# Gate and up weights of the thirty-first expert, asked for as 120 and 8 partitions

## What is computed

```python
h = rmsnorm(x, g_ffn).reshape(b * t, d)          # d = 1024
...                                               # top group, then top-2 experts in it
def add_expert(acc, params):
    wg, wu, wd, c = params                        # (1024, 512), (1024, 512), (512, 1024), float32
    act = jax.nn.silu(h @ wg) * (h @ wu)
    return acc + (act @ wd) * c[:, None], None
out, _ = lax.scan(add_expert, jnp.zeros_like(h), (w_gate, w_up, w_down, combine))
```

## Time and profile before

| | us |
|---|---|
| median of three runs | 1108.88 |
| lowest, highest | 1107.67, 1110.88 |
| the profiled execution | 1107.98 |
| its span, first to last instruction | 1106.2 |
| PE busy (share of the span) | 1052.4 (95%) |
| VectorE, ScalarE, GpSimd busy | 440.0, 235.6, 302.5 |
| HBM read, written | 290.09 MB, 29.72 MB |

### The profile page before, as it was taken

The page is one execution under the profiler, slowest core; times in us unless marked ns, Lnnn a source line. Parts: engine busy times, 40 slices in busy tenths (PEclk is TensorE's granted clock), DMA queues, the critical chain, the costliest instruction groups (busy, mean ns, idle before and its releaser), DMA issues. The chain is left out here.

```text
span 1106.2 us, 17768 instructions
## 1 busy us (share of the span) xinstructions
PE 1052.4 (95%) x6801; PEld 610.0 (55%) x6801; DVE 440.0 (40%) x1210; ACT 235.6 (21%) x545; POOL 302.5 (27%) x262
## 2 busy tenths in 40 slices
PE   6999999999999999899999999999999999988896
PEld 3644444445777777433565555555555555545453
DVE  3555888888566565523344311111111111111222
ACT  2113221122444446411021101111111111111011
POOL 1023422551554444103000112222222222222222
PEclk9999999999999999999999999999999999999999
DMA  6230232207576344897895799999999999999993
GB/s 211 92 117 21 77 106 96 94 13 273 152 237 221 118 137 141 328 387 251 336 414 201 280 357 417 413 419 414 415 413 416 417 412 415 415 417 417 418 406 123
DMA packets 85497, 304.39 MB, mean 275 GB/s; under 512 B 23453, under 2 KB 27677, under 8 KB 73507
## 3 DMA queue, kind: packets, MB, share of 16 engines
q1 hardware_dynamic: 67682, 273.47, 63.4%
q0 software_dynamic: 9824, 16.98, 5.3%
q10 hardware_dynamic: 7904, 12.78, 3.1%
HBM read 290.09 MB, written 29.72 MB: 289 GB/s over the span
## 5 line engine op out<-in xcount | busy, mean ns | idle before, releaser
L413 PE MATMUL p_z<-k_w,k_xT 128*128 128x512 f32 (+2 forms) x528 | 209.0, 550 | 0.0
L413 PEld LDWEIGHTS p_z<-k_w,k_xT 128*128 128x128 f32 (+1 forms) x528 | 92.3, 189 | 102.9 <-issue 101.7
L876 PE MATMUL a_G<-k_xT,k_w 128*128 128x260 f32 x512 | 125.9, 390 | 0.0
L2035 ACT ACTIVATE k_rows<-e_Y,x_share 64x512 f32<-64x512 f32 x64 | 43.7, 682 | 329.8 <-PE e_Y L1916 329.4
L876 PEld LDWEIGHTS a_G<-k_xT,k_w 128*128 128x128 f32 x512 | 92.2, 190 | 26.2 <-issue 13.6
L2122 DVE SCALAR_TENSOR_TENSOR k_rows<-e_G,x_share,k_rows 128x256 f32<-128x256 f32 x32 | 15.5, 484 | 228.9 <-ACT k_rows L2030 228.9
L971 POOL TENSOR_TENSOR k_x<-k_x 128x512 f32<-128x512 f32 x64 | 80.5, 1271 | 87.4 <-DVE k_side L1037 67.7
L2162 POOL DMA_INDIRECT out_y_p<-k_rows,x_table x32 | 46.2, 1444 | 176.9 <-ACT k_rows L2035 176.9
L166 POOL DMA_INDIRECT k_rows<-token_rows,x_halves x32 | 33.8, 1056 | 174.1 <-PE e_TX L1896 159.5
L1896 PEld LDWEIGHTS e_TX<-k_c,k_rows 64*64 64x64 f32 x1024 | 64.0, 212 | 13.1 <-issue 12.5
L1896 PE MATMUL e_TX<-k_c,k_rows 64*64 64x64 f32 x1024 | 68.4, 283 | 0.0
(11 more groups left out here) (375 smaller groups left out, 1549.2 us busy)
## 6 DMA issues: line engine op xcount, KB each, us to landing
k_w<-in_w_in SPq DMA_DIRECT2D x11, 2048.0 KB, 8.2
k_w<-in_w_gate SPq DMA_DIRECT2D x8, 2048.0 KB
k_w<-in_w_up SPq DMA_DIRECT2D x8, 2048.0 KB
k_xT<-in_w_down SPq DMA_DIRECT2D x8, 2048.0 KB, 27.7
k_oT<-in_w_gate SPq DMA_DIRECT2D x8, 2048.0 KB
k_side<-in_w_up SPq DMA_DIRECT2D x8, 2048.0 KB
x_page<-in_w_down SPq DMA_DIRECT2D x8, 2048.0 KB
x_w_out<-in_w_gate SPq DMA_DIRECT2D x8, 2048.0 KB
```

Source lines behind the costliest of these rows:

```text
L413: last = nc.tensor.matmul(z[u % 3][0:p, 0:WIDTH[k]], s.xT[:, j, 128 * i:128 * i + p], s.w[:, c % 2, j, 0:WIDTH[k]], start=j == 0, stop=j = ...
L876: last = nc.tensor.matmul(G[u % 2][:, 0:HT], s.w[:, q % 2, j, 128 * c:128 * c + 128], s.xT[:, j, HT * h:HT * h + HT], start=j == 0, stop=j ...
L2035: last = nc.scalar.activation(y[j][:, W * h:W * h + W], Y[j][CAP * h:CAP * h + CAP, :], ACT.Copy, scale=s.share[CAP * h:CAP * h + CAP, 0, ...
```

## The change

The thirty-first expert's gate and up weights are each asked for with two DMAs, one for partitions 0 to 119 and one for partitions 120 to 127. All other weights are asked for as before. The semaphore of the place gets 32 rather than 16 for that load, and `weights_in` adds the difference to the total that PE waits for. No byte more or less is moved, and the arithmetic is the same.

```diff
+PARTITIONS = ([slice(0, 128)], [slice(0, 120), slice(120, 128)])
+IN_FIFTEENTHS = ((NE - 2, 0), (NE - 2, 1))
+
+
 def load_expert(eng, io, s, e, n):
 
     r = e % DEPTH[n]
     for b, part in s.ew[n][r]:
-        eng.dma_start(part, s.expert(io[EXPERT_WEIGHTS[n]], e, n)[:, b:b + part.shape[1], :]).then_inc(s.ew_in[n][r], 16)
+        rows = s.expert(io[EXPERT_WEIGHTS[n]], e, n)[:, b:b + part.shape[1], :]
+        for p in PARTITIONS[(e, n) in IN_FIFTEENTHS]:
+            eng.dma_start(part[p], rows[p]).then_inc(s.ew_in[n][r], 16)
     if (n, r) == (2, FIRST):
         load_down_last(eng, io, s, e, s.ew_in[n][r])
...
 def weights_in(s, e, n):
 
     r, parts = e % DEPTH[n], len(s.ew[n][e % DEPTH[n]]) + 2 * ((n, e % DEPTH[n]) == (2, FIRST))
-    return s.ew_in[n][r], 16 * (FIRST_LOADS.get((n, r), parts) + parts * (e // DEPTH[n]))
+    parts_more = len(s.ew[n][r]) * ((e, n) in IN_FIFTEENTHS)
+    return s.ew_in[n][r], 16 * (parts_more + FIRST_LOADS.get((n, r), parts) + parts * (e // DEPTH[n]))
```

## The result

| | before | after |
|---|---|---|
| median, us (runs) | 1108.82 (4) | 1126.18 (4) |
| lowest, highest | 1107.67, 1110.88 | 1122.32, 1127.43 |
| the profiled execution | 1107.98 | 1122.32 |
| its span | 1106.2 | 1120.5 |

The change makes the kernel slower: the ratio after to before is 1.0148, 95% interval 1.0132 to 1.0165, or +17.4 us by the medians. Within the two profiled executions it is +14.3 us of span; that of after was the fastest of its four runs (the others took 1125.25 to 1127.43 us). The forecast was 1107.1 us with a range up to 1110.8.

The account below looks back on a forecast made before the run. The prediction took the slowest DMA engine's end in a full queue as the bound. A gain of 1.8 us, other terms 0, gave 1108.88 - 1.8 = 1107.1 us, range 1105.1 to 1110.8.

Parts of the forecast that it names:

- What bounds the kernel: DMA engines full from about 665 us; the slowest, about 2.4 us behind the second slowest, sets the end.
- What one partition costs: Cut gate and up loads: 0.63 us per partition; one engine spared 10.1 us, eight engines loaded 1.26 us more.
- If the spared engine is the slowest (case a): At the end of the queue, the spared engine was last: 1.1 to 2.4 us gained, 1.8 taken; chance 0.45.
- case (b): At the end of the queue, the slowest engine gets an extra partition: +1.3 us, 1110.1 us; chance 0.25.
- More instructions on SP: Two added DMA issues on SP: 0 us taken, 0 to 0.7 us if the cover is gone.
- The wait: PE waits for 16 more on two semaphores it already waits on, for the same bytes: 0 us.
- Two descriptors of completion more, and the start of small transfers: Cut loads in the full queue: between 0 and 0.63 us each, 0 taken.
- The rule against the cut: Advice of one 128-partition transfer; by it alone the cut loads would cost 1.26 us and win nothing.
- Few engines (case d): 120 partitions go to eight engines: 1119 us, share about 0.5, wait before `e_U<-x_merged` over 5 us; chance 0.07.
- The chances: For the whole kernel's measured time against before: faster 0.04, same 0.88, slower 0.08.

Follow-up runs that it names:

- e5_expert_14: The change's 120 and 8 cut on the gate and up weights of expert 14 instead of 30, against the kernel before: 1123.38 us, ratio 1.0139.
- e8_first_eight: Kernel before plus one 1 MB HBM-to-HBM copy in 8 rows behind the up load of expert 30: 1113.23 us, ratio 1.0046.
- e1_120_only: The change without its 8-partition DMAs, so partitions 120 to 127 are not loaded, against the kernel before: 1126.64 us, ratio 1.0164.
- e12_8_slices: Kernel before with the same two tensors each loaded by eight DMAs of all 128 partitions, one 2 KB row per partition each: 1108.97 us, ratio 1.0011.
- e11_2_slices: Kernel before with the same two tensors each loaded by two DMAs of all 128 partitions, rows 0-3 and 4-7: 1108.86 us, ratio 0.9997.
- e13_eight_4_apart: Kernel before with only partitions 0 to 63 of the two tensors loaded, by eight DMAs each of 8 partitions 4 apart: 1108.79 us, ratio 0.9999.

## Why the prediction was wrong, point by point

**What bounds the kernel.** Right. The rate of the full DMA queue sets the time from 665 us on, and `e5_expert_14` shows how strictly: a loss there 300 us before the end arrives at the end with 15.0 us. But the prediction went on from "a spread of engines at the end" to "that is what this change can act on". The change acted on the rate, which the prediction had fixed.

**What one partition costs.** This is the step that failed. It took 26.0 GB/s for an engine, whatever partitions it writes, and so 0.63 us for a partition. In the trace of after a busy engine has 219 / 16 = 13.7 GB/s and a partition takes 1.19 us, for 30 us. It was read from rows in which every transfer was of all 128 partitions, and no row of before showed another kind. A bound on both sides was called for: an upper end of twice the time for the two tensors alone would have been 1108.88 + 10.1 = 1119.0 us, and since the neighbours in the queue slow down too (30 us at 220 GB/s are 6.6 MB, and the two tensors are 4.2 MB), even that end is short of 1126.2.

**If the spared engine is the slowest (case a).** Wrong as the likeliest case. `e8_first_eight` places the last engine among the eight that get the extra partition, so case (b) had the right place. Its price was to be 1.3 us; of that nothing was seen, as after (1126.18 us), with the 8-partition DMAs, is no slower than `e1_120_only` (1126.64), though noise of this size could hide 1.3 us. The 17.4 us are another mechanism, and the prediction had no case for it.

**More instructions on SP.** Right: 0. The pairs of issues took 0.8 us more, and `e12_8_slices`, with fourteen issues more, stays at 1.0011.

**The wait.** Right: 0, by the same run.

**Two descriptors of completion more, and the start of small transfers.** Right: 0, by `e11_2_slices`, `e12_8_slices` and `e13_eight_4_apart`.

**The rule against the cut.** The prediction did find the advice of the Trainium skill (page "DMA: Bandwidth & Descriptors", section "Rules for kernel authors") to use one transfer of 128 partitions, and priced it at 1.26 us as the time of the small transfers. The advice was right, and its price was wrong: 64 + 64, the very cut that it names, has no small transfer and costs 20.0 us.

**Few engines (case d).** The time was the nearest, 1119, with the wrong mechanism. It asked for a share of about 0.5; the share stayed at 0.93 to 1.01. The prediction had the wait before `e_U<-x_merged` as the sign; in fact the waits were before `k_side` and `x_w_out`, and none before `x_merged`.

**The chances.** 0.88 for no difference came from cases that all moved bytes between engines at a fixed rate. The share of the cases was argued; that the list was complete was not. None of the cases let the rate of an engine change.

**What stays open.** That partitions share a way into SBUF fits the runs; no view shows a way, or an engine's number. Which partitions would share one, and at which speed, is seen here only by 4 apart against 2 or 1. An estimate in which engines that share a way divide its rate evenly gives less than was measured: half the rate for the two tensors' own 4.2 MB is +10.1 us, against 17.4; the rest would have to come from the slow packets of whole DMAs beside the cut ones, and why those are slow is not shown. And the number of partitions reached by one DMA doesn't set the size (16 or 64 neighbours, 19.2 and 20.0 us). The engines are over 20 us apart at the end, so engines at different DMAs meet; that this evens out the differences is an argument, not shown. `e12_8_slices` leaves a small thing unexplained. Its stretch from 1050 us has a lower rate (332 GB/s) at a share of 0.91, and almost no time is lost:

```profile
1050.00:1070.00 20.00, 17.04 (x142) 10.31 (x140) 5.98 (x19) 3.20 (x5) 5.29 (x4) 1.00 0.91 332
```

Its packets are of one row, 2 KB. None is missing from the trace: the page has 304.39 MB, as that of before. The bytes come later. From 1084 to 1086 us the rate is 414 GB/s, where it was 280, and the engine that ends last stops at 1095.0 us, where it stopped at 1094.3. So most of the delay fell on engines that had time to spare. Why the share is under 1 was not tried.

No version here is faster than the kernel before. The most that could be had on this path, by PE's waits, was 3.2 us.

## What to carry to other kernels

In a full queue, keep a load into SBUF at all 128 partitions: cuts into neighbouring partitions were slow here. If it must be cut, cut along the free dimension, the elements within a partition, which cost nothing that could be measured (0.9997 with two pieces, 1.0011 with eight). Read DMA share and GB/s side by side: a full share with half the rate says that the packets take longer, not that there is more work. And where a step changes the shape of a transfer in a full queue, price it by the rate of that shape, or put an upper end at twice the time and more, since its neighbours in the queue slow down with it.

## What the runs showed of the hardware

- Two 2 MB tensors, of 96 that the experts need, each cut into neighbouring partitions, slow the whole kernel by 15.0 to 20.0 us, whether as 120 + 8 (17.4), 64 + 64 (20.0), eight times 16 (19.2), or near the middle of the kernel (15.0). In the slow stretches the 16 engines move 203 to 246 GB/s, where they otherwise move 412 to 419, and a 16 KB packet takes 1.17 us (after) and not 0.61.
- Eight neighbouring partitions, or eight that are 2 apart, cost 13.5 us for 2 MB; eight that are 4 apart cost nothing (-0.1 us), with the same bytes, DMAs and packet size. While DMAs with partitions 2 or 1 apart run, packets of whole DMAs take longer as well.
- The cut into 120 and 8 between HBM and HBM costs 1.6 us by the medians, within the noise, and the rate stays at 415 GB/s.
- The engine that ends last is among the eight that a DMA of 8 rows uses: 5.04 us of added load on these came out as +4.4 us by the medians, +5.1 by the ratio. That rests on the 2.4 us between the last two engines in one execution.
